# The final norm of a decoder step, taken apart: sums normed after the 30th of 32 scatters, and the rows of the last two lists done over

## The chip, the cores and the metric

The kernel runs on one core of a Trainium2 chip. The metric is device microseconds of one execution. The program writes out by hand what each engine does and which semaphores it waits on: TensorE (PE) multiplies, VectorE (DVE) and ScalarE (ACT) work elementwise, GpSimd (POOL) issues the indirect DMAs, SyncE (SP) the direct ones.

## The reference

One step of a one-layer hybrid decoder for 1024 prompt tokens and 8 sample tokens, 1032 rows of 1024 float32 numbers. After convolution and attention branches comes a mixture of experts: each row goes to 2 of 32 experts (512 wide), and the weighted results are added to the row. A last RMS norm gives the output:

```
x = x + hier_moe(rms_norm(x, norm2_g), ...)      # each row: 2 of 32 experts
y = x * rsqrt(mean(x * x) + 1e-6) * norm_f_g     # y_prompt, y_sample
```

Each expert has its own list of rows, at most 128 in the main path (an overflow path, guarded by the count `n_ov`, handles longer lists; none is longer here). Counted from the reference's routing of its inputs, lists 29, 30 and 31 (from 0) hold 31, 57 and 53 rows.

## The kernel before

**Tiling.** Rows lie in DRAM as `(p n)`: partition p, tile n, row 9p + n, with NT = 9 tiles (the ninth has 8 rows, the sample tokens). `sum_dram` ("summed_rows") holds the residual rows; each expert's weighted output is added into it by an indirect DMA with an add.

**The experts.** The weights of an expert come in six chunks of 1 MB (two each of gate, up and down), 192 in all, loaded by SP into a ring of 12 slots (line 480) as the chunks before are used (`e_used`, counted by PE). ACT splits each chunk into a high part (line 1378, `e_hi_done`), DVE into the rest (line 1967, `e_lo_done`), and each product is three matmuls. PE works one expert ahead: in step e it does gate and up of e (lines 1059 to 1061), then the down product of e - 1 (`down_e`, `chunk_d`, line 1071) into PSUM banks 2 and 3. Before a down product PE waits until ACT has stored the previous list's rows from these banks (`y_stored`). `store_rows` (line 1408) scales them by the routing weight into `y_out`, or `y_last` for list 31.

**POOL.** For each e it gathers the rows of list e + 2 into `xg` (line 643), gathers the row weights (line 659) and scatters the rows of list e - 2 (line 651). `scatter_rows(e)` waits for `y_stored` and for the scatter before, since a row can stand in two lists. The last two scatters stand at the end, and after the last has landed POOL releases `rows_written` (line 714).

**The end.** SP, after all chunks are used, loads the gains `gfb` (line 520), waits for `rows_written`, loads nine tiles of sums into `f_out` (line 535), and stores each tile to y_prompt (line 538) or y_sample (line 540) when it is done. ACT loads the Sqrt table by a dummy operation (line 1477), then per tile takes the sum of squares (line 1481) and the root (line 1483); DVE inverts it (line 2057) and scales the tile (line 2058). Each engine works through its own list of instructions in order; a wait holds up all that is behind it.

Of the kernel before, what the change touches and what calls it, by code (L numbers as in the profile page):

```python
# [38 lines left out]
NE, NG, EG, FE = 32, 4, 8, 512  # L39
# [10 lines left out]
NOROW = 4096  # L50

ROWS = NT * P
# [54 lines left out]
def program(nc, x_prompt, x_sample, cache_conv, cache_k, cache_v, norm1_g, w_in, conv_w, w_conv_out,  # L107
# [7 lines left out]
    sum_dram = nc.dram_tensor("summed_rows", (ROWS, D), F32).ap()  # L115
# [3 lines left out]
    with ExitStack() as ctx:  # L119
        base = 16512  # L120

        def at(name, offset, shape, dt=F32):
            return nc.alloc_sbuf_tensor_at(name, [P] + shape if shape[0] != "rows" else shape[1:], dt, offset=base + offset)
# [6 lines left out]
        R3, R4, R5, RING, SMALL = 2 * W8, 3 * W8, 3 * W8 + 33856, 4 * W8 + 33856, 4 * W8 + 33856 + 36864  # L130
# [6 lines left out]
        a_lo = at("a_lo", R3, [KT, T], F32R)  # L137
        a_hi = at("a_hi", R4, [KT, T], F32R)
# [53 lines left out]
        ssq = small("ssq", [NT])  # L192
        rms = small("rms", [NT])
        eps = small("eps", [1])
# [79 lines left out]
        wl = small("wl", [NE])  # L274
        wcol = small("wcol", [1])
        warm = small("warm", [1])

        e_raw = [at(f"e_raw{i}", RING + 8192 * i if i < 4 else 8192 * (i - 4), [2048]) for i in range(12)]
        e_lo = [at(f"e_lo{i}", RING + 8192 * i if i < 4 else 8192 * (i - 4), [2048], F32R) for i in range(12)]
# [15 lines left out]
        v_xT = at("v_xT", R3, [KT, P])  # L295
        v_aT = at("v_aT", R3 + 4096, [4, P])

        f_out = at("f_out", R5, [NT, D])
        gfb = at("gfb", RING + 8192, [D])
        f_junk = at("f_junk", RING + 12288, [D])  # L300
        assert base + cur[0] <= 229344, cur[0]
# [67 lines left out]
        stage_lo, STAGE_FROM = x_scaled, 9  # L369
        rest_done, REST_FROM = h_hi_done, 16  # L370

        f_loaded, F_FROM = e_loaded[0:NT], 16 * 16

        block = ctx.enter_context(nc.Block())
# [18 lines left out]
        def _(sp):  # L393
# [122 lines left out]
            load_round(14, True)  # L516


            sp.wait_ge(e_used, 192)
            sp.dma_start(gfb[:, :], norm_f_g.partition_broadcast(P)).then_inc(gf_loaded, 16)  # L520
            sp.wait_ge(ov_sbuf, 3)
            n_ov = sp.value_load(ov_t[0:1, 2 * OVF:2 * OVF + 1], min_val=0, max_val=OVF)
            with sp.If(n_ov > 0):
                with sp.Fori(0, OVF) as i:
                    with sp.If(i < n_ov):
                        ex = sp.value_load(ov_t[0:1, bass.ds(i, 1)], min_val=0, max_val=NE - 1)
                        sp.wait_ge(v_free, i + 1)
                        for dst, w in ((v_gate, w_e_gate), (v_up, w_e_up), (v_down, w_e_down)):
                            sp.dma_start(dst[:, :, :], w[0][bass.ds(ex, 1)].rearrange("e (p k) f -> p (e k) f", p=P)).then_inc(v_loaded, 16)


            sp.wait_ge(rows_written, 1)
            for n in range(NT):
                rows = P if n < 8 else B8
                sp.dma_start(f_out[0:rows, n, :], sum_rows[0:rows, n, :]).then_inc(f_loaded[n], 16)
            with sp.Fori(0, 8) as n:
                sp.wait_ge(f_done, n + 1)
                sp.dma_start(y_prompt[0, bass.ds(n * P, P), :], f_out[:, bass.ds(n, 1), :].rearrange("p a d -> p (a d)")).then_inc(f_stored, 16)
            sp.wait_ge(f_done, 9)
            sp.dma_start(y_sample[:, 0, :], f_out[0:B8, 8, :]).then_inc(f_stored, 16)  # L540
            sp.wait_ge(f_stored, 16 * NT)
            sp.wait_ge(states_out, 16 * 7)


# [1 line left out]
        def _(pool):  # L546
# [137 lines left out]
            pool.wait_ge(idle_ready, 1)  # L684
            pool.wait_ge(ov_sbuf, 3)
            n_ov = pool.value_load(ov_t[0:1, 2 * OVF:2 * OVF + 1], min_val=0, max_val=OVF)
            for e in range(NE - 2, NE):
                scatter_rows(e)
            pool.wait_ge(scattered, 16 * NE)
            pool.sem_inc(v_free, 1)  # L690
            with pool.If(n_ov > 0):
                with pool.Fori(0, OVF) as i:
                    with pool.If(i < n_ov):
# [17 lines left out]
                        pool.wait_ge(idled, i * 2 + 2)  # L711
                        pool.wait_ge(v_scattered, i * 16 + 16)
                        pool.sem_inc(v_free, 1)
            pool.sem_inc(rows_written, 1)


        @block.tensor
        def _(pe):
# [342 lines left out]
                    mm = pe.matmul(out, xT_lo[:, par, kk, :], wh, start=False, stop=kk == KT - 1)  # L1061
                mm.then_inc(e_used, 1)

            def chunk_d(s, slot, c, a_hi=aT_hi, a_lo=aT_lo):
                pe.wait_ge(e_lo_done, s + 1)
                for k in range(2):
                    kk = 2 * (c % 2) + k
                    w_h, w_l = e_hi[:, slot % 4, :], e_lo[slot][:, :]
                    for a, w, st in ((a_hi, w_h, kk == 0), (a_hi, w_l, False), (a_lo, w_h, False)):
                        for x in range(2):  # L1070
                            mm = pe.matmul(bank[2 + x][:, :], a[:, kk, :], w[:, 1024 * k + 512 * x:1024 * k + 512 * x + 512],  # L1071
                                           start=st, stop=kk == 3 and a is a_lo)
                mm.then_inc(e_used, 1)

# [30 lines left out]

            def down_e(e, s, slot):
                pe.wait_ge(aT_lo_done, e + 1)
                if not isinstance(e, int) or e > 0:
                    pe.wait_ge(y_stored, e)
                last = isinstance(e, int) and e == NE - 1  # L1110
                parts = (last_hi, last_lo) if last else (aT_hi, aT_lo)
                chunk_d(s, slot, 0, *parts)
                if isinstance(e, int) and e == NE - 2:
                    turn_act(NE - 1)
                chunk_d(s + 1, slot + 1, 1, *parts)
# [44 lines left out]
        def _(act):  # L1160
# [238 lines left out]
            def store_rows(e, s_end, first=False):  # L1399

                act.wait_ge(e_used, s_end)
                last = isinstance(e, int) and e == NE - 1
                if not first and not last:
                    act.wait_ge(scattered, e * 16)
                dst = y_last if last else y_out
                act.wait_ge(wl_loaded, e * 16 + (WL_FROM + 16))
                for x in range(2):
                    ins = A.activation(dst[:, 512 * x:512 * x + 512], bank[2 + x][:, :], ACT.Copy, scale=wl[:, e:e + 1] if isinstance(e, int) else wl[:, bass.ds(e, 1)])
                ins.then_inc(y_stored, 1)

            def step_e(e, par, s, base, uses, first=False):
# [44 lines left out]
                step_e(i * 2 + 2, 0, i * 12 + 10, 10, i * 16)  # L1456
            step_e(31, 1, 184, 4, 240)
            a_split(31)
            store_rows(30, 190)
            store_rows(31, 192)  # L1460


            n_ov = act.value_load(ov_t[0:1, 2 * OVF:2 * OVF + 1], min_val=0, max_val=OVF)
# [10 lines left out]
                        ins.then_inc(v_y, 1)  # L1474


            A.activation(warm[:, :], eps[:, :], ACT.Sqrt)
            for n in range(NT):
                rows = P if n < 8 else B8
                act.wait_ge(f_loaded[n], F_FROM + 16)  # L1480
                A.activation(f_junk[0:rows, :], f_out[0:rows, n, :], ACT.Square, accum_out=ssq[0:rows, n:n + 1]).then_inc(f_sq, 1)
                act.wait_ge(f_sq, n + 1)
                A.activation(rms[0:rows, n:n + 1], ssq[0:rows, n:n + 1], ACT.Sqrt, bias=eps[0:rows, 0:1], scale=1.0 / D).then_inc(f_root, 1)


        @block.vector
        def _(dve):
# [536 lines left out]
            step_e(31, 1, 184, 4)  # L2024


            n_ov = dve.value_load(ov_t[0:1, 2 * OVF:2 * OVF + 1], min_val=0, max_val=OVF)
            n0 = step.n
            with dve.If(n_ov > 0):
                with dve.Fori(0, OVF) as i:  # L2030
                    with dve.If(i < n_ov):
# [15 lines left out]
            dve.wait_ge(gf_loaded, 16)  # L2047

            final = Steps(dve, final_step)

            def rows_of(n):
                return P if n < 8 else B8

            def finish(n):
                r = rows_of(n)
                dve.wait_ge(f_root, n + 1)
                final.after(V.reciprocal(rms[0:r, n:n + 1], rms[0:r, n:n + 1]))
                V.scalar_tensor_tensor(f_out[0:r, n, :], f_out[0:r, n, :], rms[0:r, n:n + 1], gfb[0:r, :], ALU.mult, ALU.mult).then_inc(f_done, 1)


            for n in range(NT):
                finish(n)


_INS = ["x_prompt", "x_sample", "cache_conv", "cache_k", "cache_v", "norm1_g", "w_in", "conv_w", "w_conv_out",
# [24 lines left out]
```

## Time and profile before

| What | Value |
|---|---|
| Median of 3 runs | 1686.56 us (1684.54 to 1686.68) |
| Profiled execution, its own time | 1685.97 us |
| Its span in the profile | 1684.4 us |
| PE busy | 1614.4 us (96%) |
| DVE, ACT, POOL busy | 1104.5 us (66%), 845.2 us (50%), 230.0 us (14%) |
| DMA traffic | 305.30 MB |

Times in the rows below are microseconds from the start of the span unless marked ns. An engine that is busy need not bound anything: what counts is the chain of waits. PE's sequencer and DMA issues are not counted as busy. PEclk is the clock granted to TensorE as a share of 2.4 GHz.

### The profile page before, as it was taken

To read this page: it belongs to the slowest core of one execution; us is meant where nothing else is said; L and a number is where in the kernel's file an instruction comes from. 1 tells how busy PE (TensorE), PEld (TensorE's weight loads), DVE (VectorE), ACT (ScalarE), POOL (GpSimd) and SP (SyncE) were. 2 spreads that over 40 slices of the span, in tenths; PEclk is the share of its full clock that TensorE was granted. 3 is DMA by queue.
4 is the path that set the end of the run, shared out by engine and by line. 5 is a ranking of instruction groups with operands and counts; after the bars stand their busy time and mean duration, and the time that the engine had idled before them with its cause. 6 is when DMAs were issued, how large, how long until landed. Compare 5 with 4: busy or idle time off the path is not lost.

```text
span 1684.4 us, 26202 instructions
## 1 busy us (share of the span) xinstructions
PE 1614.4 (96%) x9427; PEld 1471.8 (87%) x9427; DVE 1104.5 (66%) x1967; ACT 845.2 (50%) x1234; POOL 230.0 (14%) x245
## 2 busy tenths in 40 slices
PE   5999999999999999999999999799999999999992
PEld 4999999999999999999999887688888888877781
DVE  5332588888887232114214576898998998888893
ACT  6011366666665321122112211678778788778773
POOL 1111011110110000000000111322122122232310
PEclk9999999999999999999999999799999999999996
DMA  5252111111112111141113712999999999999956
GB/s 150 72 135 81 55 51 51 50 48 39 50 50 88 30 39 50 50 139 50 50 50 128 290 73 82 360 389 379 371 375 377 378 375 383 367 374 367 362 217 224
DMA packets 131856, 305.30 MB, mean 181 GB/s; under 512 B 30403, under 2 KB 92079, under 8 KB 106935
## 3 DMA queue, kind: packets, MB, share of 16 engines
q1 hardware_dynamic: 115415, 267.76, 43.4%
q0 software_dynamic: 16384, 36.76, 7.5%
q8 instruction: 37, 0.61, 0.2%
q14 instruction: 20, 0.16, 0.0%
HBM read 282.81 MB, written 40.41 MB: 192 GB/s over the span
## 4 chain that ended last, share of the span: by engine, by line
PE 87%; DMA 8%; DVE 3%; issue 1%; ACT 1%; SPq 0%; DVEq 0%; ACTq 0%; POOLq 0%
PE bank L725 10%; PE bank L727 9%; PE bank L726 9%; PE bank L1071 8%; PE bank L1059 6%; PE bank L1061 6%; PE bank L1060 5%; PE bank L871 5%; PE bank L873 5%; PE bank L872 5%; DMA e_raw<-in_w_e_gate_dram 5%; PE bank L1019 2%; PE bank L1021 2%; PE bank L1023 2%; PE bank L832 2%; DMA e_raw<-in_w_e_down_dram 1%
## 5 line engine op out<-in xcount | busy, mean ns | idle before, releaser
L1967 DVE TENSOR_TENSOR e_lo<-e_raw,e_hi 128x2048 fp32r<-128x2048 f32 x192 | 433.3, 2288 | 55.6 <-ACT e_hi L1378 40.6
L1378 ACT ACTIVATE e_hi<-e_raw 128x2048 fp32r<-128x2048 f32 x192 | 364.5, 1921 | 49.0 <-DMA e_raw<-in_w_e_gate_dram 22.2
L1167 ACT ACTIVATE w_hi<-w_raw 128x1024 fp32r<-128x1024 f32 x68 | 71.6, 1055 | 323.7 <-DMA w_raw<-in_w_in_dram 179.5
L1493 DVE TENSOR_TENSOR w_lo<-w_raw,w_hi 128x1024 fp32r<-128x1024 f32 x68 | 83.2, 1224 | 201.9 <-ACT w_hi L1167 201.8
L1059 PE MATMUL bank<-e_hi,xT_hi 128*128 128x512 f32 x512 | 205.4, 401 | 3.2 <-DVE xT_lo L1978 3.2
L725 PE MATMUL bank<-h_hi,w_hi 128*128 128x344 f32 x624 | 202.9, 325 | 1.1 <-DVE h_lo L1512 1.1
L1061 PE MATMUL bank<-e_hi,xT_lo 128*128 128x512 f32 x512 | 201.8, 394 | 0.0
L1060 PE MATMUL bank<-e_lo,xT_hi 128*128 128x512 f32 x512 | 201.1, 393 | 0.0
L726 PE MATMUL bank<-h_lo,w_hi 128*128 128x344 f32 x624 | 200.1, 321 | 0.0
L727 PE MATMUL bank<-h_hi,w_lo 128*128 128x344 f32 x624 | 200.1, 321 | 0.0
L871 PE MATMUL bank<-h_hi,w_hi 128*128 128x344 f32 x576 | 190.2, 330 | 0.0
L873 PE MATMUL bank<-h_hi,w_lo 128*128 128x344 f32 x576 | 184.2, 320 | 0.0
L872 PE MATMUL bank<-h_lo,w_hi 128*128 128x344 f32 x576 | 184.1, 320 | 0.0
L725 PEld LDWEIGHTS bank<-h_hi,w_hi 128*128 128x128 f32 x624 | 118.2, 189 | 5.0 <-issue 3.5
L1059 PEld LDWEIGHTS bank<-e_hi,xT_hi 128*128 128x128 f32 x512 | 96.2, 188 | 25.8 <-issue 5.6
L727 PEld LDWEIGHTS bank<-h_hi,w_lo 128*128 128x128 f32 x624 | 118.2, 189 | 0.0
L726 PEld LDWEIGHTS bank<-h_lo,w_hi 128*128 128x128 f32 x624 | 118.0, 189 | 0.0
L1061 PEld LDWEIGHTS bank<-e_hi,xT_lo 128*128 128x128 f32 x512 | 96.2, 188 | 23.0
L1060 PEld LDWEIGHTS bank<-e_lo,xT_hi 128*128 128x128 f32 x512 | 96.1, 188 | 20.9
L872 PEld LDWEIGHTS bank<-h_lo,w_hi 128*128 128x128 f32 x576 | 108.7, 189 | 0.0
L871 PEld LDWEIGHTS bank<-h_hi,w_hi 128*128 128x128 f32 x576 | 108.5, 188 | 0.0
L873 PEld LDWEIGHTS bank<-h_hi,w_lo 128*128 128x128 f32 x576 | 108.2, 188 | 0.0
(351 smaller groups left out, 3162.5 us busy)
## 6 DMA issues: line engine op xcount, KB each, us to landing
e_raw<-in_w_e_gate_dram SPq DMA_DIRECT2D x64, 1024.0 KB
e_raw<-in_w_e_up_dram SPq DMA_DIRECT2D x64, 1024.0 KB
e_raw<-in_w_e_down_dram SPq DMA_DIRECT2D x64, 1024.0 KB
w_raw<-in_w_in_dram SPq DMA_DIRECT2D x104, 256.0 KB, 3.3
a_spill<-y_sb POOLq DMA_DIRECT2D x8, 516.0 KB, 4.1
a_raw<-a_spill SPq DMA_DIRECT2D x2, 2064.0 KB, 13.2
x_tok<-in_x_prompt_dram SPq DMA_DIRECT2D x4, 1024.0 KB, 11.1
w_raw<-in_w_attn_out_dram SPq DMA_DIRECT2D x32, 128.0 KB, 3.0
```

What stands on the lines that cost most here:

```text
L725: pe.matmul(out, wh, xh, start=i == 0, stop=False)
L726: pe.matmul(out, wh, xl, start=False, stop=False)
L727: mm = pe.matmul(out, wl, xh, start=False, stop=i == len(pairs) - 1)
L871: pe.matmul(DN[c][:, 0:CH], w_hi[:, (s + 1) % 3, k, :], h_hi[:, k, cols], start=k == 0, stop=False)
L872: pe.matmul(DN[c][:, 0:CH], w_hi[:, (s + 1) % 3, k, :], h_lo[:, k, cols], start=False, stop=False)
L873: mm = pe.matmul(DN[c][:, 0:CH], w_lo[:, (s + 1) % 3, k, :], h_hi[:, k, cols], start=False, stop=k == KT - 1)
L1059: pe.matmul(out, xT_hi[:, par, kk, :], wh, start=kk == 0, stop=False)
L1060: pe.matmul(out, xT_hi[:, par, kk, :], wl, start=False, stop=False)
L1061: mm = pe.matmul(out, xT_lo[:, par, kk, :], wh, start=False, stop=kk == KT - 1)
L1071: mm = pe.matmul(bank[2 + x][:, :], a[:, kk, :], w[:, 1024 * k + 512 * x:1024 * k + 512 * x + 512], start=st, stop=kk == 3 and a is a_lo)
L1378: A.activation(e_hi[:, slot % 4, :], e_raw[slot][:, :], ACT.Copy).then_inc(e_hi_done, 1)
L1967: V.tensor_tensor(e_lo[slot][:, :], e_raw[slot][:, :], e_hi[:, slot % 4, :].bitcast(F32), ALU.subtract).then_inc(e_lo_done, 1)
```

## The change

SP now waits for the 30th scatter (`scattered` at 16 x 30), for 188 high parts and 184 used chunks, and then loads tiles 0 to 7 of the sums, at a time when lists 30 and 31 have not been added. These tiles are normed and stored over all of y_prompt. POOL does not issue the last two scatters until these eight loads have landed. After the last scatter it gathers the finished sums of the rows of lists 30 and 31 back from `sum_dram` into `xg`; ACT and DVE norm these two tiles, and POOL scatters them over y_prompt (a plain indirect write, the second after the first has landed; rows beyond the prompt and empty slots are skipped by the bounds check). The row numbers in y_prompt, 128 n + p from 9 p + n, are worked out on DVE by twelve small operations. Tile 8, the sample rows, is loaded only after the last scatter.

On ACT the Sqrt table and the roots of tiles 0 to 3 come between the stores of lists 30 and 31, those of tiles 4 to 7 after it. On PE the last down product goes to banks 4 and 5 and no longer waits for the store of list 30. `f_out` moves to a region that is free during the experts. If `n_ov` is over 0, all tiles are normed again after the overflow path; here it is skipped.

```diff
-        f_out = at("f_out", R5, [NT, D])
+        f_out = at("f_out", R3 + 16384, [NT, D])
@@ SP
-            sp.wait_ge(e_used, 192)
-            sp.dma_start(gfb[:, :], norm_f_g.partition_broadcast(P)).then_inc(gf_loaded, 16)
+            sp.wait_ge(e_used, 184)
+            sp.dma_start(gfb[:, :], norm_f_g.partition_broadcast(P)).then_inc(gf_loaded, 16)
+            sp.wait_ge(e_hi_done, 188)
+            sp.wait_ge(sums_begun, 16 * NT + 16)
+            sp.wait_ge(scattered, 16 * (NE - 2))
+            for n in range(8):
+                load_sums(n)
+            for n in range(8):
+                sp.wait_ge(f_done, n + 1)
+                sp.dma_start(y_prompt[0, P * n:P * n + P, :], f_out[:, n, :]).then_inc(f_stored, 16)
+            sp.wait_ge(scattered, 16 * NE)
+            load_sums(8)
+            sp.wait_ge(f_stored, 16 * 8)
+            sp.wait_ge(f_done, 11)
+            sp.dma_start(y_sample[:, 0, :], f_out[0:B8, 8, :]).then_inc(f_stored, 16)
+            sp.wait_ge(f_stored, 16 * NT)
+            sp.wait_ge(late_stored, LATE_STORED_FROM + 32)
...
-            sp.wait_ge(rows_written, 1)
-            for n in range(NT):
-                rows = P if n < 8 else B8
-                sp.dma_start(f_out[0:rows, n, :], sum_rows[0:rows, n, :]).then_inc(f_loaded[n], 16)
...
@@ POOL
+            for n in range(8):
+                pool.wait_ge(f_loaded[n], F_FROM + 16)
             for e in range(NE - 2, NE):
                 scatter_rows(e)
             pool.wait_ge(scattered, 16 * NE)
+            for b in range(2):
+                pool.indirect_dma_start(out=xg[:, b, :], out_offset=None, in_=sum_dram,
+                                        in_offset=bass.IndirectOffsetOnAxis(ap=gidx[:, NE - 2 + b:NE - 1 + b], axis=0),
+                                        bounds_check=ROWS - 1, oob_is_err=False).then_inc(late_gathered[b], 16)
+            pool.wait_ge(f_stored, 16 * 8)
+            for b in range(2):
+                pool.wait_ge(f_done, 9 + b)
+                if b == 1:
+                    pool.wait_ge(late_stored, LATE_STORED_FROM + 16)
+                pool.indirect_dma_start(out=y_prompt[0], out_offset=bass.IndirectOffsetOnAxis(ap=late_idx[:, b:b + 1], axis=0),
+                                        in_=xg[:, b, :], in_offset=None, bounds_check=S - 1, oob_is_err=False).then_inc(late_stored, 16)
+            pool.wait_ge(late_stored, LATE_STORED_FROM + 32)
@@ PE
-                if not isinstance(e, int) or e > 0:
+                if not last and (not isinstance(e, int) or e > 0):
                     pe.wait_ge(y_stored, e)
-                parts = (last_hi, last_lo) if last else (aT_hi, aT_lo)
+                parts = (last_hi, last_lo, 4) if last else (aT_hi, aT_lo)
@@ ACT
             a_split(31)
+            A.activation(warm[:, :], eps[:, :], ACT.Sqrt)
             store_rows(30, 190)
+            for n in range(4):
+                act.wait_ge(f_loaded[n], F_FROM + 16)
+                rows_root(n, n)
             store_rows(31, 192)
+            for n in range(4, 8):
+                act.wait_ge(f_loaded[n], F_FROM + 16)
+                rows_root(n, n)
+            for b in range(2):
+                act.wait_ge(late_gathered[b], LATE_FROM + 16)
+                root(xg[:, b, :], late_ss[:, b:b + 1], late_ss[:, b:b + 1], 8 + b)
+            act.wait_ge(f_loaded[8], F_FROM + 16)
+            rows_root(8, 10)
@@ DVE, after step_e(31, ...)
+            output_rows()
+            dve.wait_ge(gf_loaded, 16)
+            for n in range(8):
+                finish(n, n)
+            for b in range(2):
+                scale_rows(xg[:, b, :], late_ss[:, b:b + 1], 8 + b)
+            finish(8, 10)
```

## Rows read from the trace of the kernel before

**Rows 1.** The page's chain that ended last: shares of the span by engine.

```profile
PE 87%; DMA 8%; DVE 3%; issue 1%; ACT 1%; SPq 0%; DVEq 0%; ACTq 0%; POOLq 0%
```

**Rows 2.** The same chain in order of time, from 1636: start, us, what.

```profile
1642.31 2.78 PE bank L1071 x12
1645.08 1.40 issue
1646.49 5.80 PE bank L1071 x24
...
1653.63 0.70 issue
1654.33 6.08 DMA summed_rows<-y_last,gidx
...
1660.75 3.82 DMA f_out<-summed_rows
...
1666.38 1.28 DVE f_out L2058
...
1677.51 1.27 DVE f_out L2058
```

**Rows 3.** SP's queue: issues in order of time, then its longest last wait.

```profile
1606.28 8.68 SPq L480 DMA_DIRECT2D e_raw<-in_w_e_down_dram  x4
1652.30 0.33 SPq L520 DMA_DIRECT2D gfb<-in_norm_f_g_dram  x1
...
1678.81 0.33 SPq L540 DMA_DIRECT2D out_dram<-f_out  x1
...
SPq L119 <- DMA out_dram<-f_out: 4.8, 1, 4.8
```

**Rows 4.** Stretches: engines' busy times, then PEclk, DMA share, GB/s.

```profile
1638.50:1639.00 0.50, 0.50 (x4) 0.39 (x3) 0.50 (x1) 0.00 (x0) 0.00 (x0) 1.00 0.04 16
1639.00:1639.50 0.50, 0.50 (x4) 0.41 (x3) 0.50 (x1) 0.06 (x1) 0.00 (x0) 1.00 0.00 0
...
1656.00:1656.50 0.50, 0.00 (x0) 0.00 (x0) 0.00 (x0) 0.00 (x0) 0.00 (x0) 0.50 0.64 57
...
1659.50:1660.00 0.50, 0.00 (x0) 0.00 (x0) 0.00 (x0) 0.00 (x0) 0.00 (x0) 0.50 0.09 16
...
1664.00:1668.00 4.00, 0.00 (x0) 0.00 (x0) 1.75 (x4) 3.34 (x7) 0.00 (x0) 0.50 1.03 420
```

**Rows 5.** POOL in order of time: the scatters of lists 29 and 30.

```profile
1629.84 1.84 POOL L651 DMA_INDIRECT summed_rows<-y_out,gidx  x1 [13.06 <-ACT y_out L1408]
1647.20 1.58 POOL L651 DMA_INDIRECT summed_rows<-y_out,gidx  x1 [15.52 <-ACT y_out L1408]
```

**Rows 6.** DVE and ACT in order of time: a small cast, and the last splits and stores.

```profile
1063.38 0.16 DVE L1900 CAST adr<-adr_f 8x2 uint32<-8x2 f32 x1
...
1643.58 2.29 DVE L1967 TENSOR_TENSOR e_lo<-e_raw,e_hi 128x2048 fp32r<-128x2048 f32 x1
1645.12 1.26 ACT L1408 ACTIVATE y_out<-bank,wl 128x512 f32<-128x512 f32 x2 [2.18 <-PE bank L1071]
...
1652.31 1.26 ACT L1408 ACTIVATE y_last<-bank,wl 128x512 f32<-128x512 f32 x2 [5.92 <-PE bank L1071]
1653.59 1.28 ACT L1477 ACT_TABLE_LOAD   x1
...
1654.88 0.20 ACT L1477 ACTIVATE warm<-eps 128x1 f32<-128x1 f32 x1
```

**Rows 7.** POOL and ACT in order of time: a row-weight gather and the store it releases.

```profile
1152.51 1.01 POOL L659 DMA_INDIRECT wl<-row_weights,lst  x1 [0.31 <-issue]
...
1156.15 1.27 ACT L1408 ACTIVATE y_out<-bank,wl 128x512 f32<-128x512 f32 x2 [1.01 <-DMA wl<-row_weights,lst]
```

**Rows 8.** DMA issues: queue, operation, count, KB each, median us to landing.

```profile
gfb<-in_norm_f_g_dram SPq DMA_DIRECT2D x1, 512.0 KB, 3.3
...
out_dram<-k_out POOLq DMA_DIRECT2D x1, 128.0 KB, 2.0
```

More of the change, by code:

```diff
@@ L276, in program @@
         warm = small("warm", [1])
+        late_ss = small("late_ss", [2])
+        late_idx = small("late_idx", [2], U32)
         e_raw = [at(f"e_raw{i}", RING + 8192 * i if i < 4 else 8192 * (i - 4), [2048]) for i in range(12)]
@@ L370, in program @@
         rest_done, REST_FROM = h_hi_done, 16
+        late_gathered, LATE_FROM = gathered, 16 * (NE // 2)
+        late_stored, LATE_STORED_FROM = listed, 32 * NT
         f_loaded, F_FROM = e_loaded[0:NT], 16 * 16
@@ L516, in _, with load_sums @@
             load_round(14, True)
-            sp.wait_ge(e_used, 192)
-            sp.dma_start(gfb[:, :], norm_f_g.partition_broadcast(P)).then_inc(gf_loaded, 16)
+            def load_sums(n):
+                rows = P if n < 8 else B8
+                sp.dma_start(f_out[0:rows, n, :], sum_rows[0:rows, n, :]).then_inc(f_loaded[n], 16)
             sp.wait_ge(ov_sbuf, 3)
             n_ov = sp.value_load(ov_t[0:1, 2 * OVF:2 * OVF + 1], min_val=0, max_val=OVF)
+            sp.wait_ge(e_used, 184)
[15 more added lines that the diff above has]
+            sp.wait_ge(late_stored, LATE_STORED_FROM + 32)
             with sp.If(n_ov > 0):
@@ L529, in _ @@
                             sp.dma_start(dst[:, :, :], w[0][bass.ds(ex, 1)].rearrange("e (p k) f -> p (e k) f", p=P)).then_inc(v_loaded, 16)
-            sp.wait_ge(rows_written, 1)
-            for n in range(NT):
-                rows = P if n < 8 else B8
-                sp.dma_start(f_out[0:rows, n, :], sum_rows[0:rows, n, :]).then_inc(f_loaded[n], 16)
[L536 to L541, printed above, removed]
+                sp.wait_ge(rows_written, 1)
+                for n in range(NT):
+                    load_sums(n)
+                for n in range(8):
+                    sp.wait_ge(f_done, n + 12)
+                    sp.dma_start(y_prompt[0, P * n:P * n + P, :], f_out[:, n, :]).then_inc(f_stored, 16)
+                sp.wait_ge(f_done, 20)
+                sp.dma_start(y_sample[:, 0, :], f_out[0:B8, 8, :]).then_inc(f_stored, 16)
+                sp.wait_ge(f_stored, 32 * NT)
             sp.wait_ge(states_out, 16 * 7)
@@ L713, in _ @@
                         pool.sem_inc(v_free, 1)
-            pool.sem_inc(rows_written, 1)
+                pool.sem_inc(rows_written, 1)
         @block.tensor
@@ L1062, in chunk_gu, with chunk_d @@
                 mm.then_inc(e_used, 1)
-            def chunk_d(s, slot, c, a_hi=aT_hi, a_lo=aT_lo):
+            def chunk_d(s, slot, c, a_hi=aT_hi, a_lo=aT_lo, first_bank=2):
                 pe.wait_ge(e_lo_done, s + 1)
@@ L1070, in chunk_d @@
                         for x in range(2):
-                            mm = pe.matmul(bank[2 + x][:, :], a[:, kk, :], w[:, 1024 * k + 512 * x:1024 * k + 512 * x + 512],
+                            mm = pe.matmul(bank[first_bank + x][:, :], a[:, kk, :], w[:, 1024 * k + 512 * x:1024 * k + 512 * x + 512],
                                            start=st, stop=kk == 3 and a is a_lo)
@@ L1107, in down_e @@
                 pe.wait_ge(aT_lo_done, e + 1)
-                if not isinstance(e, int) or e > 0:
+                last = isinstance(e, int) and e == NE - 1
+                if not last and (not isinstance(e, int) or e > 0):
                     pe.wait_ge(y_stored, e)
-                last = isinstance(e, int) and e == NE - 1
-                parts = (last_hi, last_lo) if last else (aT_hi, aT_lo)
+                parts = (last_hi, last_lo, 4) if last else (aT_hi, aT_lo)
                 chunk_d(s, slot, 0, *parts)
@@ L1404, in store_rows @@
                     act.wait_ge(scattered, e * 16)
-                dst = y_last if last else y_out
+                dst, b0 = (y_last, 4) if last else (y_out, 2)
                 act.wait_ge(wl_loaded, e * 16 + (WL_FROM + 16))
                 for x in range(2):
-                    ins = A.activation(dst[:, 512 * x:512 * x + 512], bank[2 + x][:, :], ACT.Copy, scale=wl[:, e:e + 1] if isinstance(e, int) else wl[:, bass.ds(e, 1)])
+                    ins = A.activation(dst[:, 512 * x:512 * x + 512], bank[b0 + x][:, :], ACT.Copy, scale=wl[:, e:e + 1] if isinstance(e, int) else wl[:, bass.ds(e, 1)])
                 ins.then_inc(y_stored, 1)
@@ L1458, in _, with root, rows_root @@
             a_split(31)
+            A.activation(warm[:, :], eps[:, :], ACT.Sqrt)
             store_rows(30, 190)
-            store_rows(31, 192)
+            def root(src, ss, out, count):
+                A.activation(f_junk[0:src.shape[0], :], src, ACT.Square, accum_out=ss).then_inc(f_sq, 1)
+                act.wait_ge(f_sq, count + 1)
+                A.activation(out, ss, ACT.Sqrt, bias=eps[0:src.shape[0], 0:1], scale=1.0 / D).then_inc(f_root, 1)
+            def rows_root(n, count):
+                r = P if n < 8 else B8
+                root(f_out[0:r, n, :], ssq[0:r, n:n + 1], rms[0:r, n:n + 1], count)
+            for n in range(4):
+                act.wait_ge(f_loaded[n], F_FROM + 16)
+                rows_root(n, n)
+            store_rows(31, 192)
+            for n in range(4, 8):
[6 more added lines that the diff above has]
+            rows_root(8, 10)
             n_ov = act.value_load(ov_t[0:1, 2 * OVF:2 * OVF + 1], min_val=0, max_val=OVF)
@@ L1474, in _ @@
                         ins.then_inc(v_y, 1)
[L1477 to L1483, printed above, removed]
+                A.activation(warm[:, :], eps[:, :], ACT.Sqrt)
+                for n in range(NT):
+                    act.wait_ge(f_loaded[n], F_FROM + 32)
+                    rows_root(n, n + 11)
         @block.vector
@@ L2024, in _, with output_rows, scale_rows, finish @@
             step_e(31, 1, 184, 4)
+            late = Steps(dve, final_step)
+            def output_rows():
+                f, q, n, g = lst_f[:, 0:2], lst_f[:, 2:4], lst_g[:, 0:2], lst_g[:, 2:4]
+                late.after(V.tensor_copy(f, gidx[:, NE - 2:NE]))
+                late.after(V.tensor_scalar(q, f, 1.0 / NT, -4.0 / NT, ALU.mult, ALU.add))
+                late.after(V.tensor_copy(late_idx[:, :], q))
+                late.after(V.tensor_copy(q, late_idx[:, :]))
+                late.after(V.scalar_tensor_tensor(n, q, -float(NT), f, ALU.mult, ALU.add))
+                late.after(V.tensor_scalar(g, n, float(NT), 1.0, ALU.is_ge, ALU.mult))
+                late.after(V.tensor_tensor(q, q, g, ALU.add))
+                late.after(V.scalar_tensor_tensor(n, g, -float(NT), n, ALU.mult, ALU.add))
+                late.after(V.scalar_tensor_tensor(n, n, float(P), q, ALU.mult, ALU.add))
+                late.after(V.tensor_scalar(g, f, float(ROWS), float(NOROW), ALU.is_ge, ALU.mult))
+                late.after(V.tensor_tensor(n, n, g, ALU.add))
+                late.after(V.tensor_copy(late_idx[:, :], n))
+            def scale_rows(rows, root, count):
+                r = rows.shape[0]
+                dve.wait_ge(f_root, count + 1)
+                late.after(V.reciprocal(root, root))
+                V.scalar_tensor_tensor(rows, rows, root, gfb[0:r, :], ALU.mult, ALU.mult).then_inc(f_done, 1)
+            def finish(n, count):
+                r = P if n < 8 else B8
+                scale_rows(f_out[0:r, n, :], rms[0:r, n:n + 1], count)
+            output_rows()
+            dve.wait_ge(gf_loaded, 16)
+            for n in range(8):
+                finish(n, n)
+            for b in range(2):
+                scale_rows(xg[:, b, :], late_ss[:, b:b + 1], 8 + b)
+            finish(8, 10)
             n_ov = dve.value_load(ov_t[0:1, 2 * OVF:2 * OVF + 1], min_val=0, max_val=OVF)
@@ L2043, in _ @@
                         V.tensor_copy(v_aT[:, :, :], bank[6][:, :].rearrange("p (k t) -> p k t", k=4)).then_inc(v_aT_done, 1)
[L2047 to L2062, printed above, removed]
+                for n in range(NT):
+                    finish(n, n + 11)
 _INS = ["x_prompt", "x_sample", "cache_conv", "cache_k", "cache_v", "norm1_g", "w_in", "conv_w", "w_conv_out",
```

## The prediction

> **What bounds the kernel now.** I read the page's chain first: it is PE for 87% of the span and DMA for 8% [rows 1], so nearly everything is matmul, and this change touches only what follows the last weights. So I took the chain over the last 48 us [rows 2]. The reader is to see that TensorE's last product ends near 1652.3 and that the remaining 32 us are a relay: output row store, last accumulating scatter (6.08 us, landed 1660.41), load of the first sums (3.82), first norm, then nine scalings at a pace of (1677.51 - 1666.38) / 8 = 1.39 us. The queue of SP [rows 3] shows the rest: the last store is issued at 1678.81 and SP waits 4.8 us for it, to 1683.9; the span ends 0.5 later. The stretches [rows 4] show what that tail costs: DMA at share 1.03 and 420 GB/s from 1664 on, and none at all from 1639.0 to 1645. Eight sums of 512 KB in and out are 8.4 MB, some 20 us at that rate, and they sit behind the last scatter while the queues had stood idle before it. From the last scatter's landing to the end is 1684.4 - 1660.4 = 24.0 us. The change can shorten this relay, and replaces it by another one; the sum compares the two.
>
> **Part by part.** T is the landing of the last scatter. Scatters and stores are counted from 1: the 31st is that of list 30.
>
> 1. *When the sums can start.* SP now waits for the 30th scatter. It starts at 1629.84 [rows 5]; with the last one's 6.08 us it lands at 1635.9. Bounds: 1634, as it carries 31 rows instead of 53, and 1639.0, where the last DMA traffic ends [rows 4]. I take 1636. The other waits (188 splits, 184 chunks) end before.
>
> 2. *The eight loads.* The first landed 3.82 us after its issue [rows 2]; seven more of 512 KB at 420 GB/s are 1.25 each: 1636.3 + 3.8 + 8.8 = 1648.9. But in 1638.5 to 1639.0 a share of 0.04 is still busy, about one of 16 engines, and its part of the loads stands behind its last weights: 1639.0 + 8 x 1.25 + 0.5 = 1649.5. I take 1649.3 (1648 to 1651.4, the last for a scatter landing at 1639). The weights are not delayed: all were issued by 1615 [rows 3], ahead on the same queue. The load of the gains moves from 1652.3 to about 1627, costs a 0.33 us issue, and is hidden.
>
> 3. *The wait put on POOL.* Scatters 31 and 32 now stand behind all eight loads, on POOL's in-order queue. From release to start POOL took 0.75 (0.70 "issue" and two small pieces) [rows 2]: scatter 31 starts at 1650.05 instead of 1647.20 [rows 5]: 2.85 later. This is the new cost on the path.
>
> 4. *The last product.* Banks 4 and 5 take away the 1.40 us in which PE waited for store 31 [rows 2]; TensorE ends near 1650.9. I cost it at nothing: scatter 32 now waits for scatter 31, not for y_last. Without that cover it would give up to 1.4.
>
> 5. *ACT's new order.* The Sqrt table (1.28 + 0.20) moves into the 2.18 us in which ACT idled before store 31 [rows 6]: hidden. Four roots follow at no more than 1.39 each, from 1646.4 to 1651.9, their loads landed (the fourth near 1644.5). Then y_last, 1.26 us, ends at 1653.2 instead of 1653.6. Scatter 32 can't use it before 1657, so 4 us of slack cover it; loads later than that by 4 us would make y_last late.
>
> 6. *DVE.* Twelve tiny operations on 128x2, at 0.16 us and a short step between (a CAST, [rows 6]), about 2.4 us in all, begin after the last split ends at 1645.87: done at 1648.3, while the first root arrives at 1648.0. Nothing. Eight scalings then end near 1660, the eight stores are issued by 1660.3 and land by about 1664: also before the gathers end.
>
> 7. *Two scatters in a row.* Alone: 1650.05 + 6.1, 0.75, 6.1 give T = 1663.0. But the y_prompt stores (512 KB each 1.39 us, 1.25 of DMA time) now run at the same time, where before the queues were nearly free. A contended accumulating scatter is not shown in the trace. Below: nothing extra, since a row-weight gather on POOL's queue, issued amid weight traffic, released ACT within 1156.15 - 1152.51 = 3.64 us [rows 7]. Above: if the scatter's data time of 4 us (1656.0 to 1660) is doubled, 4.0 each. I take 1.0 each, near the row-weight gather. T = 1665.0, 4.6 later than before.
>
> 8. *The new relay.* From T: 0.75 to the gather's start, G to its landing, 3.1 to its scaled rows (the chain from 1664.57 to 1667.66), 0.75 to the output scatter, S, 0.75, S again (the second waits for the first), 0.5 to the end. G and S, indirect transfers without an accumulate of 57 and 53 rows (the reference's routing of its inputs), are not in the trace at an idle time. Bounds: from below 2.0, POOL's direct store of 128 KB [rows 8], above the accumulating 6.08. Nearest by kind is the row-weight gather, 3.64, plus some 0.3 for a quarter of a megabyte: I take 4.0 for each. Sum: 0.75 + 4.0 + 3.1 + 0.75 + 4.0 + 0.75 + 4.0 + 0.5 = 17.85.
>
> By the fit in the Trainium skill ("DMA: Bandwidth & Descriptors", Anatomy of one DMA) a POOL DMA takes about 2.0 us plus its bytes over 436 GB/s, an estimate of 2.5 here; the sum would then be 4.5 lower. The row-weight gather of 512 bytes at 3.64 speaks against it.
>
> 9. *Beside it.* The ninth load goes out at T, its root behind the two late ones, its store near T + 11.2: 6 us under cover of the scatters. The overflow block is jumped over, as before: nothing.
>
> **Sum:** 4.6 (T later) + 17.85 - 24.0 = -1.55 us. The profiled execution took 1685.97 (span 1684.4), so 1684.4; it is 0.6 below the median of the three runs, 1686.56, so against that median 1685.0. A measurement of this kernel can tell about 0.2%, 3.4 us, from no change; the forecast is therefore no change, with 1683 (no contention) to 1688 (contention of 2 each, loads 1 us later) as its own range.
>
> **Rivals.**
> *Quick indirect transfers (faster).* G and S land in 2.7, between the 2.0 and the 3.3 of the direct transfers of [rows 8]: 3 x 1.3 = 3.9 less, so -5.4, or 1681. For it: the list holds a quarter of a megabyte and the DMA queues are then idle. Against it: 3.64 for a tiny indirect one. It decides from G + 2S under 10.1. The skill's fit, above, is on its side.
>
> *The stores starve the accumulating scatters (slower).* In 1650 to 1663 each row of the scatter is read, added and written back on the same engines through which y_prompt goes. The scatter's data time of 4 us takes a share between 0.64 and under 0.1 [rows 4], so it is made of latencies; if each row also has to wait for a store's packet on both legs, 4 us become 8: 3 more per scatter than I took, +6, in all +4.5, or 1691. Against it: the gather amid weights at 3.64. It decides from 9.6 us per scatter on. The Trainium skill ("DMA: Bandwidth & Descriptors", Queues, rings and completion order) says that each engine takes turns between queues packet by packet, which speaks for some of this; no run here shows it for an accumulate.
>
> *The early start isn't early.* If the 30th scatter lands only at 1639, with the last traffic, the loads end at 1651.4, the sum is +0.5, 1687: still no change.
>
> **How the numbers follow.** Forecast with the late start: 0.62; quick transfers 0.26; starved scatters 0.12. The first lies within 3.4 us, the others give the signs. The range 1681.3 to 1688.8 takes in the quick case to about its price and the forecast with contention of 2 each; left out are most of the starved case and the lowest part of the quick one.
>
> **What would show it.** Right: loads of the sums issued near 1636 and DMA share near 1 in 1638 to 1649; scatter 31 starting near 1650 and 32 near 1658, later than before, with POOL waiting for f_out loads; T near 1665; PE's 1.40 gone; the gathers and two output scatters one after the other ending the chain, about 4 us each. Wrong: scatter 31 starting at 1647 or after 1653 (step 2), an interval between scatters far from 7.9 (step 7), indirect transfers under 3 or over 5 (step 8), or a chain that ends with y_sample or y_prompt.

## The result, and the profile after

The changed kernel takes 1691.5 us (median of 6 runs, 1691.12 to 1692.14), the kernel before 1686.62 (6 runs, 1683.18 to 1688.38): a ratio of 1.0035, 95% interval 1.0025 to 1.0045. It is slower by about 0.35%. The forecast was no change, 1685.0, with a range up to 1688.8: the result lies beyond it, on the slower side.

The spans of two executions differ by a few microseconds already where the code is the same, so I count from one instruction that the change does not touch, ACT's store of list 30 (`y_out`, [rows 6]). In the kernel before it starts at 1645.12 and the span ends 39.28 us later; with the change it starts at 1645.43 and the end comes 44.67 us later: 5.39 more.

The chain of waits of the changed kernel over its last 60 us (start, us, what):

```profile
1630.19 8.92 DMA summed_rows<-y_out,gidx
1639.11 0.02 issue
...
1642.76 9.25 DMA f_out<-summed_rows
1652.00 0.02 issue
...
1653.07 7.57 DMA summed_rows<-y_out,gidx
...
1661.45 6.91 DMA summed_rows<-y_last,gidx
...
1669.16 4.08 DMA xg<-summed_rows,gidx
1673.24 0.02 issue
1673.27 1.16 ACT f_junk L1497 x2
...
1674.97 1.30 DVE xg L2101
...
1677.14 3.36 DMA out_dram<-xg,late_idx
1680.50 0.02 issue
...
1681.37 0.99 POOL out_dram L721
```

Against [rows 2] and [rows 5]: the gap of 1.40 us on TensorE is gone from the chain, and so are the nine scalings. In their place stand the 30th scatter (8.92 us), the loads that wait for it and the two scatters that wait for the loads, then the gather, the norm and the two output scatters. Scatter 31 starts at 1653.07 instead of 1647.20; the last scatter lands at 1668.36 instead of 1660.41.

The chain stops at 1682.4, 7.7 us ahead of the end of the span. What comes there stands in SP's waits (the engine and line that waited, what for, us in total, times, longest):

```profile
SPq L545 <- DMA out_dram<-xg,late_idx: 4.3, 1, 4.3
SPq L119 <- PEq L119: 5.0, 1, 5.0
```

The first is the landing of the second output scatter, near 1684.6. The second is the block's end, line 119, where all engines meet. GpSimd's instructions on that line, in the changed kernel (count, ns min/median/max, first and last start):

```profile
L119 POOLq DRAIN  x1: 4971/4971/4971, 1684.9 to 1684.9; - x1
```

and in the kernel before:

```profile
L119 POOLq DRAIN  x1: 4644/4644/4644, 1660.8 to 1660.8; - x1
L119 SPq DRAIN  x1: 13/13/13, 1684.2 to 1684.2; - x1
```

GpSimd closes its program with a DRAIN of nearly 5 us; SP's takes 13 ns. Before, GpSimd was done at 1660.8 and its DRAIN ran under the norm. With the change GpSimd is the last to end, and the DRAIN stands in the open. The wait is put down to PE's sequencer by the profile, but GpSimd's DRAIN fills the same time, 1684.9 to 1689.9.

### The profile page after: what moved, and what is told of

Its sections match the earlier page's. It is cut to its first block, busy times and chain, and to the rows that moved or that the text cites. A ratio compares the mean times of both kernels' runs of the same rounds, so it can differ in the third digit from the quotient of the medians.

```text
span 1690.1 us, 26196 instructions
## 1 busy us (share of the span) xinstructions
PE 1613.5 (95%) x9427; PEld 1470.9 (87%) x9427; DVE 1109.1 (66%) x1983; ACT 848.0 (50%) x1240; POOL 238.4 (14%) x249
## 4 chain that ended last, share of the span: by engine, by line
PE 85%; DMA 9%; DVE 2%; issue 1%; ACT 1%; SPq 0%; POOL 0%; POOLq 0%; DVEq 0%; ACTq 0%
PE bank L759 10%; PE bank L761 9%; PE bank L760 9%; PE bank L1105 7%; DMA e_raw<-in_w_e_gate_dram 6%; PE bank L905 5%; PE bank L907 5%; PE bank L1093 5%; PE bank L906 5%; PE bank L1095 5%; PE bank L1094 5%; PE bank L1053 2%; PE bank L1055 2%; PE bank L1057 2%; PE bank L866 2%
```

## The experiments

All times of a run below are of its profiled execution; "counted from the store" means from the start of `y_out` for list 30. Runs 3 to 7 leave out work or load other values, so their output is not the reference's, and each was executed once: what they show is read from one trace each. In the code, `...` stands for lines left out, and comments are added for the reader.

**1. Does the DRAIN cost as much whenever GpSimd ends late?** One wait added to the kernel before.

```diff
             pool.sem_inc(rows_written, 1)
+            pool.wait_ge(f_stored, 16 * NT)
```

> The kernel before, with one wait more: GpSimd does not end its program until all nine output tiles are stored. Theory 1 (GpSimd's closing DRAIN, 4.64 us in the trace of before and there under cover of the norm, takes that long whenever its program ends): the DRAIN starts when the last store has landed, near 1684, and the span grows by 4.6 to 5.0 us, to about 1689. Rival (the 4.64 us was GpSimd settling the scatters that it had just issued, so a late end with nothing in flight is quick): the span grows by under 0.5 us.

```profile
L119 POOLq DRAIN  x1: 4644/4644/4644, 1683.3 to 1683.3; - x1
```

The span ends 43.8 us after the store (1644.27 to 1688.1), 4.55 more than before; the ratio to before is 1.0029 (1.0017 to 1.0040). Nothing had been in flight on GpSimd's queue for over 20 us, so this DRAIN is not the settling of scatters: theory 1 holds, the rival (under 0.5 us) is out, and one wait with no work behind it makes the old kernel nearly as slow as the changed one.

**2. Can the DRAIN run beside the last landing?** GpSimd's last wait taken away.

```diff
-            pool.wait_ge(late_stored, LATE_STORED_FROM + 32)
             pool.sem_inc(v_free, 1)
```

> The changed kernel without GpSimd's last wait, the one for the landing of the second output scatter, which SP waits for as well. Theory 1 (a fixed DRAIN from the end of the program): GpSimd ends at about 1682.4, as soon as the scatter is issued, its DRAIN runs beside the landing and ends near 1687.4, and the span is 1687.6, 2.5 us shorter than with the change. Rival (the DRAIN waits for what GpSimd has issued): it ends at the landing plus 4.6 to 5 us, no change from 1690.1.

```profile
L119 POOLq DRAIN  x1: 7496/7496/7496, 1681.2 to 1681.2; - x1
```

The DRAIN starts with the scatter, but takes 7.5 us, to 1688.7, some 4.3 after the scatter's landing (SP's wait for it ends near 1684.4). Counted from the store the end is 43.9, 0.75 less than with the change, not 2.5; over the six executions there is no gain (median 1690.33, ratio to before 1.0036). Here the rival is nearer: it looks as if what GpSimd has in flight were waited for first. That is not shown apart from a DRAIN that simply takes longer behind a fresh scatter. Both runs together: about 4.3 to 5 us from the moment at which GpSimd has ended and its DMAs have landed, whichever is later.

**3. What does the late part cost?**

```diff
-            for b in range(2):
-                pool.indirect_dma_start(out=xg[:, b, :], ... in_=sum_dram, ...)
...
-                pool.indirect_dma_start(out=y_prompt[0], ... in_=xg[:, b, :], ...)
-            pool.wait_ge(late_stored, LATE_STORED_FROM + 32)
...
-                root(xg[:, b, :], late_ss[:, b:b + 1], late_ss[:, b:b + 1], 8 + b)
-                scale_rows(xg[:, b, :], late_ss[:, b:b + 1], 8 + b)
...
```

> The changed kernel without its late part: the rows of the last two lists are not gathered, normed and scattered over the output (their first values stay). GpSimd ends after the last scatter. Theory (the relay of gather, norm and two scatters is 16.2 us and the DRAIN after it 5.0): the last scatter lands at 1668.4 as with the change; then only the sample tile is left, 2.5 for its load, 3.1 for the norm, 2.3 for its store, under which the DRAIN is hidden; span near 1677. Rival (something else at the end of the program sets it): span over 1682.

The span is 1674.4 (1677 was expected): 30.0 us after the store, against 44.7 with the change and 39.3 before. The DRAIN, again 4644 ns, runs from 1667.4 under the sample tile's load, norm and store. So norming 1024 rows early is worth 9.3 us; putting the last two lists right costs 14.7, 5.0 of it the DRAIN.

**4. Do the tile stores slow the accumulating scatters?**

```diff
             for n in range(8):
                 sp.wait_ge(f_done, n + 1)
-                sp.dma_start(y_prompt[0, P * n:P * n + P, :], f_out[:, n, :]).then_inc(f_stored, 16)
...
-            sp.wait_ge(f_stored, 16 * 8)
...
-            pool.wait_ge(f_stored, 16 * 8)
```

> The changed kernel without the eight stores of whole tiles to y_prompt, and without the waits for them; only the rows of the last two lists and the sample rows are written. Theory (the accumulating scatters are slowed by the tile stores beside them, 7.57 and 6.91 us against 6.08 before): both take 6.1 again and the last scatter lands 2.3 us earlier, at 1666.1, the span 2.3 us shorter. Rival (the stores cost them nothing; the lists or the loads do): intervals of 7.6 and 6.9 as with the change, span 1690.

GpSimd in order of time (start, us of descriptor work, operation, idle before):

```profile
1652.95 1.57 POOL L669 DMA_INDIRECT summed_rows<-y_out,gidx  x1 [20.72 <-issue]
1659.77 2.26 POOL L669 DMA_INDIRECT summed_rows<-y_last,gidx  x1 [5.25 <-DMA summed_rows<-y_out,gidx]
1667.21 1.06 POOL L711 DMA_INDIRECT xg<-summed_rows,gidx  x1 [5.18 <-DMA summed_rows<-y_last,gidx]
```

In the chain of waits the scatters take 6.01 and 6.64 (the second with 2.26 us of descriptor work instead of 1.55). Counted from the store the last lands 2.2 earlier, the span ends 2.3 earlier, as expected: the stores cost the relay about 2.3 us. Of it 1.8 is in the two scatters and 0.4 in the loads, which land that much earlier.

**5. What sets the landing of the loads?**

```diff
-                sp.dma_start(f_out[0:rows, n, :], sum_rows[0:rows, n, :]).then_inc(f_loaded[n], 16)
+                sp.dma_start(f_out[0:rows, n, :], (xn_rows if n < 8 else sum_rows)[0:rows, n, :]).then_inc(f_loaded[n], 16)
...
-            sp.wait_ge(scattered, 16 * (NE - 2))
```

> The changed kernel with its eight early tiles loaded from the normed rows instead of the sums, so that SP need not wait for the 30th scatter; it starts them after 188 splits, near 1633. GpSimd's wait for these loads stays. The values of the output are not the reference's. Theory (some DMA engines still work off weights until 1639, and their parts of the loads stand behind these): the loads land only at 1649.5 to 1650, 2 to 2.5 us earlier than the 1652.0 with the change, although issued 6 us earlier, and the span shortens by as much. Rival (the loads take 12.6 us from issue whenever they are issued): they land at 1646, scatter 31 starts at 1647.2, the span shortens by 5.9 us.

The first load is issued at 1631.88, 7.3 us earlier than with the change (8.0 counted from the store), and the last lands at 1651.76. Stretches of one microsecond (the last columns are granted clock, DMA share, GB/s):

```profile
1642.00:1643.00 1.00, 0.50 (x4) 0.37 (x4) 0.58 (x1) 0.41 (x1) 0.00 (x0) 1.00 1.04 426
...
1646.00:1647.00 1.00, 1.00 (x6) 0.82 (x5) 0.96 (x3) 0.89 (x2) 0.00 (x0) 1.00 0.21 86
...
1649.00:1650.00 1.00, 1.00 (x6) 0.83 (x5) 0.93 (x3) 0.97 (x3) 0.00 (x0) 1.00 0.06 25
1650.00:1651.00 1.00, 1.00 (x6) 0.78 (x6) 0.96 (x3) 1.00 (x3) 0.00 (x0) 1.00 0.06 25
```

Most of the DMA engines are done by 1645 (share 0.23 in that microsecond); from then on the share falls to 0.06, as much as one of 16 engines, at 25 GB/s, and it is this rest that the last load waits for. The rival (1646) is out. With the change itself no such rest is seen: there the share is near 1 from 1642 on, also in the last microsecond before the first tile store is issued (1649.99):

```profile
1649.00:1650.00 1.00, 1.00 (x6) 0.83 (x5) 1.00 (x2) 0.97 (x4) 0.00 (x0) 1.00 1.03 414
```

A part of the loads that is behind the others fits the theory, its size does not: counted from the store the loads land only 0.9 us earlier than with the change, not 2 to 2.5. That this part stands behind weights is not shown. The span, 46.0 after the store, is 1.3 longer (its first output scatter took 4.85 us instead of 3.36, its two accumulating ones 0.8 more). Starting the loads sooner buys nearly nothing.

**6. And if GpSimd doesn't wait for them?** The edits of run 5, and this one on top:

```diff
-            for n in range(8):
-                pool.wait_ge(f_loaded[n], F_FROM + 16)
             for e in range(NE - 2, NE):
                 scatter_rows(e)
```

> As the run before (tiles loaded from the normed rows), and GpSimd does not wait for the loads either. Theory (the wait for the loads is the cost of the change on the path): scatter 31 starts at 1647.4 instead of 1653.1, the last scatter lands about 5.7 us earlier, near 1662.7, less what the loads beside it take (up to 1.5), and the span shortens by 4.2 to 5.7 us, to 1684.4 to 1686. Rival (scatters beside the loads are slowed as much as they gain): span 1688 or more.

```profile
1644.18 1.57 POOL L670 DMA_INDIRECT summed_rows<-y_out,gidx  x1 [15.54 <-ACT y_out L1439]
1650.94 1.55 POOL L670 DMA_INDIRECT summed_rows<-y_last,gidx  x1 [5.19 <-DMA summed_rows<-y_out,gidx]
```

The store stands at 1642.10 here, so scatter 31 starts 2.08 after it, as before the change, and the span ends 40.3 after it, 4.4 less than with the change: within the theory's 4.2 to 5.7. The last scatter lands 5.7 earlier; the gather and the output scatters behind it took 1.3 longer. Against run 5, from which this run differs by the wait alone, the end is 5.7 earlier. The second scatter, beside the tile stores, takes 8.38.

**7. Why did the 30th scatter take 8.92 us?**

```diff
-                    load_chunk(c, cc, i * 2 + (1 + de), i * 12 + (1 + c))
+                    load_chunk(c, cc, i * 2 + (1 + de), i * 12 + (1 + c), final and c >= 8)   # half the chunk
...
```

> The changed kernel with the last four chunks of weights (down weights of the last two lists) loaded, split and multiplied by halves only, 2 MB of weights less; the values of the last two lists are not the reference's. Theory (the 30th scatter lands at 1639.1 because its last packets share engines that work off weights until then): the weights end near 1634.5 and the scatter lands at 1635 to 1636, the loads at 1648 to 1649. Rival (a scatter of 31 rows beside any traffic takes 8.9 us by itself): it lands at 1639 again.

```profile
1627.64 5.96 DMA summed_rows<-y_out,gidx
...
1633.68 0.33 SPq L526
```

The splits and the products of these chunks are halved as well. With half of the last weights the same scatter lands after 5.96 us, about the 5.7 to 6.1 of a scatter on idle queues; with all of them it took 8.92 to 8.94 in the changed kernel and three of the runs above, and 8.9 in runs 1 and 8 too, which are built on the kernel before. It is the weights still in the queues that held it. The loads then take 12.47 us from first issue to last landing (1633.68 to 1646.15), and the prediction had 12.6.

**8. The own banks alone, in the kernel before.**

```diff
-                if not isinstance(e, int) or e > 0:
+                if not last and (not isinstance(e, int) or e > 0):
                     pe.wait_ge(y_stored, e)
-                parts = (last_hi, last_lo) if last else (aT_hi, aT_lo)
+                parts = (last_hi, last_lo, 4) if last else (aT_hi, aT_lo)
...
```

> The kernel before with one part of the change alone: the last down product in banks 4 and 5, without the wait for the store of list 30. Theory (the last scatter waits for the one before it, which lands near 1653.3): the 1.40 us gap of TensorE goes, y_last is stored at 1652.2, and the last scatter starts only 0.3 us earlier, at 1654.0; no change that can be measured. Rival (it waits for y_last): it starts 1.4 us earlier, at 1652.9, span 1683.0.

```profile
1648.80 1.58 POOL L651 DMA_INDIRECT summed_rows<-y_out,gidx  x1 [15.51 <-ACT y_out L1408]
1655.35 1.55 POOL L651 DMA_INDIRECT summed_rows<-y_last,gidx  x1 [4.97 <-DMA summed_rows<-y_out,gidx]
```

The ratio is 0.9994 (0.9985 to 1.0004): nothing that can be measured. The two scatters start 6.55 apart instead of 7.13, and the second now waits for the landing of the first instead of ACT.

**9. and 10. A version without the costs found.** Lists 30 and 31 no longer go into the summed rows, so that nothing waits for the loads.

```diff
-            for n in range(8):
-                pool.wait_ge(f_loaded[n], F_FROM + 16)
-            for e in range(NE - 2, NE):
-                scatter_rows(e)
+            pool.wait_ge(scattered, 16 * (NE - 2))
+            for b in range(2):                                   # rows of both lists, with 30 lists in them
+                pool.indirect_dma_start(out=xg[:, b, :], ... in_=sum_dram, ...)
...
+            pool.wait_ge(y_stored, NE - 1)
+            pool.indirect_dma_start(out=late_dram, ... in_=y_out[:, :], ...)      # plain
...
+            add_late(0, y_out)
...
+            pool.indirect_dma_start(out=late_add[:, :], ... in_=late_dram, ...)   # rows in both lists
...
+            add_late(1, y_last)
...
+            add_late(1, late_add)
...
```

> A version made from what the runs showed. Lists 30 and 31 are no longer added into the summed rows, so GpSimd waits for no load: their rows are gathered right after the 30th scatter, the products are added in SBUF by GpSimd (rows that stand in both lists get the first product by a second DRAM table, written by a plain scatter and gathered back), normed, and scattered over the output after the tile stores; the sample rows likewise. It keeps GpSimd as the last to end. Theory (the cost of the change was the wait for the loads, two accumulating scatters behind it, and the DRAIN): loads end near 1653, tile stores land near 1664, the two output scatters one after the other near 1672.5, the DRAIN 5.0 after that: span 1677 to 1679, 6 us under before. Rival (the added gathers and GpSimd's adds delay the loads or the late rows as much): span 1684 or more.

It gained nothing: 1691.64 us, ratio 1.0036 (1.0023 to 1.0049). But the end comes 39.0 us after the store, as in the kernel before; the loss lies ahead of it, for the store starts at 1651.03 instead of 1644 to 1647 in most of the others. Most of that loss arises where the second table is filled, in one go, from 932.0 on: in 960 to 970 the DMA share is 1.01 and TensorE is busy for 6.65 us, against 0.26 and 10.00 in the kernel before, and GpSimd's store of rows in that stretch starts 5.1 us later (963.68 against 958.57), where it was 1.3 behind ahead of the filling. And behind the store VectorE is stretched (GpSimd's and VectorE's rows in order of time):

```profile
1663.36 2.65 POOL L720 TENSOR_TENSOR xg<-xg,y_last 128x1024 f32<-128x1024 f32 x1
```

```profile
1663.91 3.19 DVE L2146 SCALAR_TENSOR_TENSOR f_out<-f_out,rms,gfb 128x1024 f32<-128x1024 f32 x1
1667.21 1.28 DVE L2146 SCALAR_TENSOR_TENSOR f_out<-f_out,rms,gfb 128x1024 f32<-128x1024 f32 x1
```

A scaling beside an addition on GpSimd took 3.19 us, the next one 1.28. The stretched one ends 1.1 us after the addition does (1667.10 and 1666.01), as if it had been held until then. So the additions went to VectorE and the filling of the second table (4.7 MB) was spread out:

```diff
-            pool.dma_start(late_dram[0:S, :]..., x_prompt[0]...).then_inc(list_blank, 16)
+            for n in range(NT):
+                pool.wait_ge(chunk_out, 114 + 5 * n)
+                pool.dma_start(late_dram[P * n:P * n + P, :], x_prompt[0, ...]).then_inc(list_blank, 16)
...
-                pool.tensor_tensor(xg[:, b, :], xg[:, b, :], part[:, :], ALU.add).then_inc(late_sum, 1)
+                V.tensor_tensor(xg[:, b, :], xg[:, b, :], part[:, :], ALU.add).then_inc(late_sum, 1)
```

> The version before, mended where its trace showed a loss: the second DRAM table is filled in nine pieces spread over the projections instead of in one go ahead of the router, the three additions of products are made by VectorE instead of GpSimd, the tile stores come before them, and GpSimd ends when its last scatter is issued. Theory (the version before lost 5.6 us ahead of the last list to the filling of the table, and 6 us to VectorE operations stretched beside GpSimd's additions): the store of list 30 starts at 1645 again, the tile stores land near 1666, the last scatter near 1674, the DRAIN ends near 1679: 5 us under before, ratio 0.997. Rival (the tail is bound by the 9 MB that go in and out, however ordered): the end is 39 us or more after the store of list 30, as before, no change that can be measured.

1683.12 us against 1685.26 (11 and 15 runs), ratio 0.9986 (0.9977 to 0.9995): faster than the kernel before by about 0.14%, and so faster than the changed one. The store is back at 1646.94, and the end comes 36.4 after it, 2.9 less than before. The expected 5 us were not reached: the chain of waits, then GpSimd's line at the block's end, show where the rest is.

```profile
1664.41 5.10 DMA out_dram<-f_out
...
1670.31 4.03 DMA out_dram<-xg,late_idx
```

```profile
L120 POOLq DRAIN  x1: 7331/7331/7331, 1675.7 to 1675.7; - x1
```

The last tile store lands at 1669.5, the first output scatter at 1674.3, and the DRAIN ends at 1683.0, some 4.2 us after SP has seen the last landing, near 1678.8.

## Why the prediction was wrong

Counted from the store, step by step; the forecast's sum was T (the landing of the last scatter) 4.6 later, a relay of 17.85, 24.0 saved. Its three chances add up to 1, so it left nothing for a cost that stood in none of its steps.

- **The end, step 8: the step that failed.** "0.5 to the end" was taken from the kernel before, where GpSimd had ended 23 us ahead. It measured 5.5 (1684.6 to 1690.1), with a DRAIN of 4.97 us in it. The 4.64 us DRAIN stood in the trace of before, on line 119 of GpSimd's sequencer, and I had read only the engines' work and SP's waits; I asked what each moved step costs, but not what follows the program of the engine that now ends last. Runs 1 and 3 show it in both directions: +4.55 us in the old kernel by a wait alone, hidden again where GpSimd ends early. Without this one term the sum would be +0.4 and the result "no change". The Trainium skill ("VectorE: DVE Perf Modes", The DRAIN you can't avoid) tells of a closing DRAIN of about 12 ns, constant on all five engines. SP's 13 ns here agrees; GpSimd's 4644 to 5216 ns does not, and the measurement decides.
- **T, steps 1 and 2: 3.0 us later than forecast,** 2.7 of it in the start of scatter 31; the prediction's own sign against step 2, a start after 1653, came (1653.07). I took 1636 for the landing of the 30th scatter, by the 6.08 us of a scatter on idle queues, with 1639.0 as the upper bound; it landed at 1639.11. This bound was the right reading: run 7 shows that the weights still in the queues hold the scatter. The loads then took 12.8 us from their first issue, as worked out, and the third rival, priced at loads ending at 1651.4, is what happened (1652.0). Alone it would not have changed the verdict, as forecast. The Trainium skill ("DMA: Bandwidth & Descriptors", Queues, rings and completion order, and Why a DMA increments its semaphore by 16 and not by 1) has every engine take turns between its queues, and a DMA complete only when the last of its engines has. Run 5, with a share of 0.06 left for the last microseconds, agrees with the second; the first no run here shows by itself.
- **POOL's wait, step 3: right.** Scatter 31 starts at the landing of the loads plus 1.07 (0.75 and the waits), and run 6 puts a price on it: 4.4 us of the span against the changed kernel, 5.7 against run 5.
- **Contention, step 7: right in size.** 1.0 for each was taken; it measured 1.5 and 0.8 (7.57 and 6.91 against 6.08), and 1.8 for both by run 4. Not all of the 1.5 need be traffic: the descriptor work of that scatter on GpSimd took 2.52 us instead of 1.58, and in run 2, where it took 1.57, the scatter took 7.16. The starved scatters, at 9.6 or more, did not occur, though the sign of that rival did.
- **The relay, step 8: slightly high.** The gather took 4.08 and the first output scatter 3.36, where 4.0 was taken for each; from T to the landing of the second it was 16.2, and 17.35 was forecast. So the quick rival, with 2.7 for each, is out. The prediction's 4.0 was 3.64 "plus some 0.3 for a quarter of a megabyte"; that 0.3 no row shows, and at the 420 GB/s of [rows 4] it would be 0.6. The estimate of 2.5 by the Trainium skill ("DMA: Bandwidth & Descriptors", Anatomy of one DMA) is too low for both.
- **Own banks, ACT, VectorE, steps 4 to 6: hidden, as forecast.** Run 8 measured nothing for the banks; y_last was stored by 1653.3, 8 us ahead of its scatter; the twelve index operations took 2.4 us.

Together: -1.55, +3.0 for T, -1.1 for the relay, +5.0 for the DRAIN, which is +5.35, and 5.39 was measured. The relay's -1.1 hid a part of T's 3.0.

## What to carry to other kernels

Ask which engine ends last after a change, and read the closing instructions of that engine in the trace: GpSimd's DRAIN cost 4.2 to 5.2 us here from the point at which GpSimd had ended and its last DMA had landed, so a kernel's end should not hang on GpSimd unless that is gained back. A load that may start earlier need not land earlier (0.9 us for 8.0 here); look at the DMA share of the last microseconds ahead of its landing, not at its mean. And a wait that guards a buffer against a new early reader is paid by everything behind it on that queue: 4.4 to 5.7 us here.

## What the runs showed of the hardware that was not expected

GpSimd's closing DRAIN took 4.64 us with nothing in flight in four kernels, 4.97 in five that ended with the output scatters landed (5.22 in run 9), and 7.3 to 7.5 where a scatter was still under way. What it does in that time no run shows. A scaling on VectorE of 1.28 us took 3.19 beside an elementwise addition on GpSimd. And the loads of the tiles ended within a microsecond of each other (counted from the store) whether their first was issued at 1632 or at 1639: in the first case as much as one of 16 DMA engines was behind the others for the last two microseconds, in the second the share was near 1 until the tile stores joined. Why a part is behind was not tried.
